# Loads, norm sums, reloads and reads moved around the dense stages of a two-block layer kernel

## The chip, the cores and the metric

The kernel runs on one core of one Trainium2 chip. The metric is the device time of one execution in microseconds (us); lower is better. TensorE does the matmuls, VectorE, ScalarE and GpSimd the elementwise work, and SyncE (SP) issues most of the loads. Every engine runs its own list of instructions in order and waits on semaphores for the others.

## The reference, cut to what matters

The input is x (1024 tokens of 1024 features, float32), with weights for five layers in a row. In short:

```
h = rmsnorm(x) @ w_in                  # split into 9 parts
oa = gated linear recurrence (4 heads) ; ob = banded attention (8 heads)
x = x + (sigmoid(ga)*(oa@wa) + sigmoid(gb)*(ob@wb)) @ w_out      # merge, wout
x = x + (silu(h2@w_gate) * (h2@w_up)) @ w_down                   # gu, dn
x = x + sigmoid(h3@w_ple_gate) * (p@w_ple_proj)                  # pleg
u = rmsnorm(x) @ w_in_a ; y = lru(conv(u[:1280])) * silu(u[1280:])
x = x + y @ w_out_a                                              # xg, wo1, wo2
c_kv, k_rope = split(rmsnorm(x)@w_dkv) ; cq, gate = split(rmsnorm(x)@w_in_b)
x = x + (causal attention with low-rank q, k, v * silu(gate)) @ w_out_b
out = rmsnorm(x) * final_norm
```

An rmsnorm multiplies each token by 1/sqrt(mean of its squares + eps) and each feature by a gain.

## The kernel before

All activations are kept transposed, as [128 features, chunk, 1024 tokens], eight chunks for the 1024 features. Tokens are worked on in two halves h of 512. A product of float32 is made from a high and a low part: ScalarE rounds a chunk to `..H` (ACT.Copy, with the norm's gain as scale), VectorE makes `..L` = x*gain - H, GpSimd splits each weight unit of 128x1024 in the same way (`split`), and TensorE does three matmuls of 128x128 by 128x512 per chunk and half: wH by H, wH by L, wL by H. The factor 1/rms of a token is not multiplied into the input but into the result, when VectorE reads it from PSUM. So a stage can begin before its norm is known, but the first read of its results cannot: the squares are made by ScalarE, added up chunk by chunk by VectorE in `square_sum` (acc), summed over the partitions by TensorE with a matrix of ones (`norm`), and turned into rstd by ScalarE with Ln and Exp.

The order of the stages is the table STREAM: za0, za1, zv, gates0, zqk, gates1, gates2, merge, wout, gu0 to dn2, proj, pleg, xg, wo1, wo2, dkv, cq, cgate, the attention's units, wob. A stage has units; a unit is one weight tile and gives 128 features, 48 matmuls for eight chunks. Units alternate between two pairs of PSUM banks, 0 and 1 or 2 and 3, so a unit can only start when VectorE has read the unit but one before it (`s_free`). Weights alternate between two slots too: `load_unit(u)` on SP waits for the split of unit u-2, and the split for the matmuls of unit u-2.

Five places matter here.

- The start. SP loads weight unit 0, then x in four DMAs of two chunks (`s_x`). ScalarE first waits for `s_const`, which counts the constants vectors, identity and ones. TensorE does unit 0 of za0, then `norm(0, 0)`, then units 1 to 7.
- The gates. Results of gates2 are staged in `gates_staged_late` and stored to DRAM by `store_gates` on SP, in between the loads. The tile shares its bytes with chunk 3 of `o_band_low` (obL), so before VectorE writes that chunk it waits for the last stores (`s_gst`), and TensorE waits for the chunk (`s_ol`) ahead of the second part of the first merge unit. ScalarE, when gates2 is done, issues one DMA of 4 MB for x_mid.
- The end of the recurrent layer. `rnn_block(n)` on VectorE reads unit (n, 0) of xg, does the convolution of block n, `recurrence(n - 1)`, reads unit (n, 1) into rnn_gate, and makes `y_low(n - 1)`. Behind the loop come the reads of the first two units of wo1, `recurrence(9)`, `y_low(9)`, and the other reads. The residual x_late is loaded again by ScalarE's queue behind its loop.
- wo2 and dkv. `split_x(4, ...)` adds the results of wo2 to x_late and sums its squares; `split_x(5, ...)` then makes the parts of h_kv, `split_x(6, ...)` behind the norm those of h_mla, and VectorE reads dkv behind all of them.
- The last norm. `split_x(7, ...)`, `norm(5, 7)` and `norm_rstd(5)` follow the last unit of wob; then come eight products x_out of 1024 tokens, and four stores.

The regions R(0) to R(4) of 32 KB per partition hold one tensor of eight chunks each.

## Time and profile before

| | us |
|---|---|
| median of 3 runs (2760.71 to 2761.88) | 2760.83 |
| the profiled execution | 2760.46 |
| its span | 2758.5 |
| TensorE busy | 2638.1 |
| VectorE busy | 1273.2 |
| ScalarE busy | 768.5 |
| GpSimd busy | 879.1 |

The span is from the first to the last instruction or landing that was recorded; the execution's own time is 1.96 us longer. Busy times of engines overlap. Only what delays TensorE, or lies ahead of its first or behind its last matmul, shows in the time.

### The profile page before, as it was taken

The page shows a single profiled execution, that of the slowest core. Times are in us where ns is not written, and L with a number is a line of the kernel's source. Part 1 is how long each engine was busy: PE and PEld are TensorE (multiplying, and loading weights), DVE is VectorE, ACT ScalarE, POOL GpSimd, SP SyncE. Part 2 cuts the span into 40 slices and gives each one's busy share as a digit, 9 for nine tenths or more (in the row PEclk, how much of TensorE's full clock was granted, in tenths as well). Part 3 has the DMA queues.
Part 4 walks back from the last instruction along what each step waited for, and adds up shares of the span by engine and source line. Part 5 has one row for each costly group of instructions (what it writes and reads, how often), then busy time and mean ns, then how long its engine had stood idle before and what let it go on. Part 6 is the DMA issues. An engine that isn't in the chain of part 4 may idle for free.

```text
span 2758.5 us, 33222 instructions
## 1 busy us (share of the span) xinstructions
PE 2638.1 (96%) x13008; PEld 2179.0 (79%) x13008; DVE 1273.2 (46%) x1584; ACT 768.5 (28%) x1005; POOL 879.1 (32%) x660
## 2 busy tenths in 40 slices
PE   6999999899899999999999999999999899999996
PEld 5888887677688888888888877788877677888875
DVE  4474633466454322122212374668864323555543
ACT  5144244222221200000000122355531321444421
POOL 3453523211233333333333352333345223111111
PEclk9999999999999999999999999999999899999998
DMA  3101121111431111111111121211132211000021
GB/s 121 47 29 39 39 77 39 46 39 46 153 126 58 46 53 46 46 51 48 46 53 46 46 83 62 103 46 38 46 114 77 101 54 36 19 19 16 24 84 68
DMA packets 44498, 160.71 MB, mean 58 GB/s; under 512 B 4720, under 2 KB 9072, under 8 KB 41968
## 3 DMA queue, kind: packets, MB, share of 16 engines
q1 hardware_dynamic: 38336, 124.53, 13.4%
q10 hardware_dynamic: 6064, 34.78, 3.3%
q8 instruction: 72, 1.18, 0.2%
q14 instruction: 26, 0.21, 0.0%
HBM read 138.33 MB, written 20.97 MB: 58 GB/s over the span
## 4 chain that ended last, share of the span: by engine, by line
PE 84%; DVE 8%; ACT 4%; issue 3%; DMA 1%; ACTq 0%; DVEq 0%
PE ps L561 17%; PE ps L562 17%; PE ps L563 17%; PE ps L626 5%; PE ps L628 5%; PE ps L627 5%; PE ps L1004 2%; PE ps L691 1%; PE ps L786 1%; PE ps L806 1%; PE ps L994 1%; PE ps L794 1%; PE ps L922 1%; PE ps L924 1%; PE ps L923 1%
## 5 line engine op out<-in xcount | busy, mean ns | idle before, releaser
L441 POOL TENSOR_TENSOR derived_vectors<-w_staged 1x1 f32<-1x1 f32 x208 | 50.4, 242 | 1784.2 <-PE ps L563 1083.3
L444 POOL TENSOR_TENSOR w_low<-w_staged,w_high 128x1024 fp32r<-128x1024 f32 x208 | 557.3, 2679 | 16.7
L561 PE MATMUL ps<-h_ffn_high,w_high 128*128 128x512 f32 x832 | 324.6, 390 | 1.6 <-DVE ple_proj L1827 1.6
L563 PE MATMUL ps<-h_ffn_high,w_low 128*128 128x512 f32 x832 | 323.7, 389 | 0.0
L562 PE MATMUL ps<-h_ffn_low,w_high 128*128 128x512 f32 x832 | 323.7, 389 | 0.0
L626 PE MATMUL ps<-h_mix_high,w_high 128*128 128x512 f32 x688 | 282.1, 410 | 0.0
L628 PE MATMUL ps<-h_mix_high,w_low 128*128 128x512 f32 x688 | 269.1, 391 | 0.0
L627 PE MATMUL ps<-h_mix_low,w_high 128*128 128x512 f32 x688 | 268.4, 390 | 0.0
L442 POOL CAST w_high<-w_staged 128x1024 fp32r<-128x1024 f32 x208 | 215.0, 1034 | 0.0
L1809 DVE TENSOR_TENSOR squares<-ps,rstd 128x512 f32<-128x512 f32 x88 | 60.5, 688 | 322.1 <-PE ps L563 311.7
L561 PEld LDWEIGHTS ps<-h_ffn_high,w_high 128*128 128x128 f32 x832 | 156.2, 188 | 34.7 <-issue 2.5
L562 PEld LDWEIGHTS ps<-h_ffn_low,w_high 128*128 128x128 f32 x832 | 156.2, 188 | 32.8 <-issue 0.5
L563 PEld LDWEIGHTS ps<-h_ffn_high,w_low 128*128 128x128 f32 x832 | 156.2, 188 | 32.5
L628 PEld LDWEIGHTS ps<-h_mix_high,w_low 128*128 128x128 f32 x688 | 129.2, 188 | 28.1
L627 PEld LDWEIGHTS ps<-h_mix_low,w_high 128*128 128x128 f32 x688 | 129.7, 189 | 25.4 <-issue 1.5
L626 PEld LDWEIGHTS ps<-h_mix_high,w_high 128*128 128x128 f32 x688 | 129.8, 189 | 25.4 <-issue 1.5
L561 PE MATMUL ps<-act_high,w_high 128*128 128x512 f32 x352 | 136.9, 389 | 0.0
L562 PE MATMUL ps<-act_low,w_high 128*128 128x512 f32 x352 | 136.9, 389 | 0.0
L563 PE MATMUL ps<-act_high,w_low 128*128 128x512 f32 x352 | 136.9, 389 | 0.0
L561 PE MATMUL ps<-h_rnn_high,w_high 128*128 128x512 f32 x320 | 125.0, 391 | 1.6 <-DVE h_rnn_low L1452 1.6
L1479 DVE TENSOR_TENSOR x_mid<-ps,x_mid 128x512 f32 (+1 forms) x64 | 43.2, 686 | 178.2 <-PE ps L563 178.2
L563 PE MATMUL ps<-h_rnn_high,w_low 128*128 128x512 f32 x320 | 124.5, 389 | 0.0
(342 smaller groups left out, 5362.3 us busy)
## 6 DMA issues: line engine op xcount, KB each, us to landing
w_staged<-weights_in SPq DMA_DIRECT2D x200, 512.0 KB, 3.4
gates_loaded<-gates ACTq DMA_DIRECT2D x8, 1024.0 KB, 7.3
gates<-gates_staged_late SPq DMA_DIRECT2D x24, 256.0 KB, 2.0
x_in<-xT_in SPq DMA_DIRECT2D x4, 1024.0 KB, 9.4
x_mid<-xT_in ACTq DMA_DIRECT2D x1, 4096.0 KB, 12.9
x_spill_rnn<-x_mid ACTq DMA_DIRECT2D x8, 512.0 KB, 2.6
x_late<-x_spill_rnn ACTq DMA_DIRECT2D x4, 1024.0 KB, 7.8
x_spill_mla<-x_late ACTq DMA_DIRECT2D x1, 4096.0 KB, 11.1
```

What stands on the lines that cost most here:

```text
L441: nc.gpsimd.tensor_tensor(derived[0:1, 72:73], w_staged[0:1, j, 0:1], w_staged[0:1, j, 0:1], ALU.add)
L442: nc.gpsimd.tensor_copy(w_high[:, j], w_staged[:, j]).then_inc(s_wh, 1)
L444: nc.gpsimd.tensor_tensor(w_low[:, j], w_staged[:, j], f32(w_high[:, j]), ALU.subtract).then_inc(s_split, 1)
L561: nc.tensor.matmul(ps[:, bank], wH, rhs[0][:, r, tok], start=(n == 0), stop=False)
L562: nc.tensor.matmul(ps[:, bank], wH, rhs[1][:, r, tok], start=False, stop=False)
L563: last = nc.tensor.matmul(ps[:, bank], wL, rhs[0][:, r, tok], start=False, stop=last_chunk)
L626: nc.tensor.matmul(ps[:, bank], wH, h1H[:, c, tok], start=(c == 0), stop=False)
L627: nc.tensor.matmul(ps[:, bank], wH, h1L[:, c, tok], start=False, stop=False)
L628: done = nc.tensor.matmul(ps[:, bank], wL, h1H[:, c, tok], start=False, stop=(c == DC - 1))
L1004: last = nc.tensor.matmul(ps[:, 6, 0:P], v_mla[H // 2 % 2][:, k, (H % 2) * P:(H % 2 + 1) * P], mla.probsT[:, n % 2, k * P:(k + 1) * P], st ...
L1479: read(stage, i, j, h, lambda p: nc.vector.tensor_tensor(xm, p, xm, ALU.add))
L1809: read(stage, m, part, h, lambda p: nc.vector.tensor_tensor(sq[:, part, half_of(h)], p, rstd[:, half_of(h)], ALU.mult))
```

## The change

It has six parts.

1. Start: x comes in eight DMAs of one chunk with semaphores of their own, ScalarE and VectorE wait for vectors alone, the constant far_mask is dropped, and the first norm's sum stands behind the second unit of za0.
2. Gates: the stores of the last unit of gates2 are issued by ScalarE ahead of x_mid, no longer by SP.
3. Recurrent layer: the last block is taken out of the loops. In it VectorE reads the last unit of xg ahead of `recurrence(8)`, and ScalarE issues the reload of x_late behind the high part of the convolution.
4. wo2 and dkv: h_kv_high is made chunk by chunk behind the squares, and the low parts of chunks 0 to 3 behind the sums, within wo2. To have room, regions 1 and 4 change places for the tensors of the last layer, and the low parts lie four chunks further on (`low_chunk`). VectorE makes four low parts of h_mla, reads unit 0 of dkv, makes the other four, and reads on.
5. End: the last unit's square, sum, rstd, products and stores are done by halves of tokens; the sum of half 0 stands within the last unit (`between`).
6. Some semaphores have other names or are gone (s_invT, s_qnH).

```diff
 # SyncE
             for k in range(4):
-                sp.dma_start(x1[:, 2 * k:2 * k + 2], a["xT"][:, 2 * k:2 * k + 2]).then_inc(s_x[k], 16)
+                sp.dma_start(x1[:, 2 * k], a["xT"][:, 2 * k]).then_inc(s_xe[k], 16)
+                sp.dma_start(x1[:, 2 * k + 1], a["xT"][:, 2 * k + 1]).then_inc(s_x[k], 16)
...
-                    if 0 <= t < STAGE[stage][2]:
+                    if 0 <= t < min(STAGE[stage][2], 9):
                         store_gates(stage, t)
...
-            for h in range(4):
-                sp.wait_ge(s_fin, 2 * (h + 1))
-                sp.dma_start(a["outT"][:, 2 * h:2 * h + 2], out_sb[:, 2 * h:2 * h + 2]).then_inc(s_out, 16)
-            sp.wait_ge(s_out, 4 * 16)
+            for h in range(2):
+                for k in range(4):
+                    sp.wait_ge(s_fin, DC * h + 2 * (k + 1))
+                    sp.dma_start(a["outT"][:, 2 * k:2 * k + 2, half_of(h)], out_sb[:, 2 * k:2 * k + 2, half_of(h)]).then_inc(s_out, 16)
+            sp.wait_ge(s_out, 8 * 16)
 # TensorE
-            pe.wait_ge(s_const, 48)
             pe.wait_ge(s_split, 1)
             tile("za0", 0, 0, 0, P, 0, [(c, c) for c in range(DC)], (h1H, h1L), low(0))
+            unit_of("za0", 1)
+            pe.wait_ge(s_const, 32)
             norm(0, 0)()
-            for t in range(1, 8):
+            for t in range(2, 8):
                 unit_of("za0", t)
...
-            gemm("dkv", (h5H, h5L), low(5), norm(4, 4))
+            def kv_ready(r):
+                return (s_l, 32 + r + 1) if r < 4 else (s_l, 40 + r - 4 + 1)
+
+            gemm("dkv", (h5H, h5L), kv_ready, norm(4, 4), low_chunk=lambda r: (r + 4) % DC)
...
-            gemm("wob", (y7H, y7L), lambda r: (s_y7l, r + 1))
-            norm(5, 7)()
+
+            def last_sum(h):
+                pe.wait_ge(s_fsum, h + 1)
+                nc.tensor.matmul(ps[:, 4 + h], ones[:], acc[:, half_of(h)], start=True, stop=True).then_inc(s_nsum, 1)
+
+            gemm("wob", (y7H, y7L), lambda r: (s_y7l, r + 1), between_last=lambda: last_sum(0))
+            last_sum(1)
 # ScalarE
-            act.wait_ge(s_const, 48)
+            act.wait_ge(s_vec, 16)
             for m in range(DC):
-                act.wait_ge(s_x[m // 2], 16)
+                act.wait_ge((s_x if m % 2 else s_xe)[m // 2], 16)
...
+            for h in range(2):
+                act.wait_ge(s_free[bank_of("gates2", 9, h)], use_of("gates2", 0, 9) + 1)
+                act.dma_start(a["gates"][gate_unit("gates2", 9)][:, half_of(h)], gates_late[:, h]).then_inc(s_gst[h], 16)
             act.wait_ge(s_mm, MM_PER_UNIT * STAGE["merge"][0])
             act.dma_start(x2[:], a["xT"]).then_inc(s_x2, 16)
...
+            def x_reloaded():
+                act.wait_ge(s_mm, mm_count("xg", 2 * RB - 1, 1))
+                for k in range(4):
+                    act.dma_start(x4[:, 2 * k:2 * k + 2], a["x_spill_rnn"][:, 2 * k:2 * k + 2]).then_inc(s_x[k], 16)
...
                 nc.scalar.activation(convH[:], conv[:], ACT.Copy).then_inc(s_ch, 1)
+                if isinstance(n, int) and n == RB - 1:
+                    x_reloaded()
                 if not static:
                     y_high(n - 1)
...
-            split_x(4, x4, None, 0, updated("wo2"))
-            split_x(5, x4, h5H, G_KV, None, False)
+            split_x(4, x4, h5H, G_KV, updated("wo2"))
             norm_rstd(4)
-            split_x(6, x4, h6H, G_B, None, False)
+            split_x(5, x4, h6H, G_B, None, False)
...
-            split_x(7, x5, None, 0, updated("wob"))
-            norm_rstd(5)
+            split_x(6, x5, None, 0, updated("wob"), late=4, n=DC - 1)
+            act.wait_ge(s_l, 52 + 6)
+            for h in range(2):
+                act.wait_ge(s_free[bank_of("wob", 1, h)], use_of("wob", 3, 1) + 1)
+                nc.scalar.activation(sq[:, 1, half_of(h)], x5[:, DC - 1, half_of(h)], ACT.Square).then_inc(s_fsq, 1)
+                nc.scalar.activation(derived[0:1, 73:74], eps[0:1], ACT.Ln)
+                act.wait_ge(s_nsum, 2 * 5 + h + 1)
+                inverse_root([(rstd[:, half_of(h)], ps[:, 4 + h], 1.0 / D, s_rstd)])
 # VectorE
+                if last:
+                    project(n, 1, rgate)
                 if not first:
                     recurrence(n - 1)
-                project(n, 1, rgate)
+                if not last:
+                    project(n, 1, rgate)
...
-            split_x(4, x4, None, None, 0, add_to("wo2", x4))
-            split_x(5, x4, h5H, h5L, G_KV, squares=False)
+            def kv_low(m):
+                return nc.vector.scalar_tensor_tensor(out=h5L[:, (m + 4) % DC], in0=x4[:, m], scalar=V(G_KV + m), in1=f32(h5H[:, m]),
+                                                      op0=ALU.mult, op1=ALU.subtract)
+
+            for m in range(DC):
+                add_to("wo2", x4)(m // 2, m % 2)
+                dve.wait_ge(s_h, 32 + m + 1)
+                if m == 0:
+                    last = nc.vector.tensor_copy(acc[:], sq[:, 0])
+                else:
+                    dve.wait_ge(s_l, 32 + m)
+                    last = nc.vector.tensor_tensor(acc[:], acc[:], sq[:, m % 2], ALU.add)
+                if m < 4:
+                    last = kv_low(m)
+                last.then_inc(s_l, 1)
+            for m in range(4, DC):
+                kv_low(m).then_inc(s_l, 1)
...
+            query_low(0, 4)
             norm_rstd(4)
-            split_x(6, x4, h6H, h6L, G_B, squares=False)
...
+                    if k == 0 and t == 1:
+                        query_low(4, DC)
...
+            for h in range(2):
+                xm = x5[:, DC - 1, half_of(h)]
+                read("wob", 3, 1, h, lambda p: nc.vector.tensor_tensor(xm, p, xm, ALU.add))
+                dve.wait_ge(s_fsq, h + 1)
+                nc.vector.tensor_tensor(acc[:, half_of(h)], acc[:, half_of(h)], sq[:, 1, half_of(h)], ALU.add).then_inc(s_fsum, 1)
+            for h in range(2):
+                dve.wait_ge(s_rstd, 2 * 5 + h + 1)
+                for m in range(DC):
+                    nc.vector.scalar_tensor_tensor(out=out_sb[:, m, half_of(h)], ...)
```

TensorE's list around the first norm; rows 128x512 of h_mix are matmuls of za0, L609 and L611 the sum with ones. Before, behind the 48 matmuls of unit 0:

```order
L562 MATMUL ps<-h_mix_low,w_high 128x512
L563 MATMUL ps<-h_mix_high,w_low 128x512
L609 MATMUL ps<-square_sum,ones 128x512 x2
L626 MATMUL ps<-h_mix_high,w_high 128x512
L627 MATMUL ps<-h_mix_low,w_high 128x512
```

Afterwards the same sum stands behind 96:

```order
L629 MATMUL ps<-h_mix_low,w_high 128x512
L630 MATMUL ps<-h_mix_high,w_low 128x512
L611 MATMUL ps<-square_sum,ones 128x512 x2
L628 MATMUL ps<-h_mix_high,w_high 128x512
L629 MATMUL ps<-h_mix_low,w_high 128x512
L630 MATMUL ps<-h_mix_high,w_low 128x512
```

The sum has moved behind the 48 matmuls of unit 1.

VectorE's list at the end of the loop over the blocks of the recurrent layer, with the last lines of the loop's body. Before, the scan and the product of the recurrence come ahead of the two reads of rnn_gate:

```order
L1857 SCALAR_TENSOR_TENSOR rnn_r<-rnn_in,rnn_i 128x1024
L1859 REGISTER_ALU
L1861 REGISTER_ALU
L1861 TENSOR_TENSOR rnn_gate<-rnn_r,rnn_gate 128x1024
L1462 ISA
L1846 REGISTER_ALU
L1846 TENSOR_TENSOR rnn_gate<-ps,rstd 128x512
L1462 REGISTER_ALU
L1846 REGISTER_ALU
L1846 TENSOR_TENSOR rnn_gate<-ps,rstd 128x512
L1436 TENSOR_TENSOR rnn_y_low<-rnn_gate,rnn_y_high 128x1024
```

Afterwards, in the last block behind the loop, the two reads come ahead of the recurrence; the reads of wo1 into x_late are still behind it, and most of them behind the next one:

```order
L1458 TENSOR_TENSOR rnn_conv_low<-rnn_conv,rnn_conv_high 128x1024
L1868 TENSOR_TENSOR rnn_gate<-ps,rstd 128x512 x2
L1874 SCALAR_TENSOR_TENSOR rnn_r<-rnn_in,rnn_r 128x1024
L1877 TENSOR_TENSOR rnn_i<-rnn_i,rnn_r 128x1024
L1879 SCALAR_TENSOR_TENSOR rnn_r<-rnn_in,rnn_i 128x1024
L1883 TENSOR_TENSOR rnn_gate<-rnn_r,rnn_gate 128x1024
L1458 TENSOR_TENSOR rnn_y_low<-rnn_gate,rnn_y_high 128x1024
L1501 TENSOR_TENSOR x_late<-ps,x_late 128x512 x2
```

The reads of rnn_gate have moved from behind the recurrence to ahead of it; nothing else in the order of this place has.

VectorE's list between wo2 and cq. Before, eight low parts of h_mla (two, and a loop) stand ahead of the reads of dkv into squares (this tile holds the latent ckv there) and tmp:

```order
L1452 SCALAR_TENSOR_TENSOR h_mla_low<-x_late,vectors,h_mla_high 128x1024 x2
L143 UNCONDITIONAL_BRANCH
L143 ISA
L1452 ISA x2
L1452 SCALAR_TENSOR_TENSOR h_mla_low<-x_late,vectors,h_mla_high 128x1024
L1444 REGISTER_ALU
L1452 ISA x2
L1452 SCALAR_TENSOR_TENSOR h_mla_low<-x_late,vectors,h_mla_high 128x1024
L143 REGISTER_ALU
L143 COMPARE_AND_BRANCH
L1918 TENSOR_TENSOR squares<-ps,rstd 128x512 x4
```

Afterwards, behind the last sum, four low parts of h_kv, four of h_mla, the reads of unit 0, and the other four:

```order
L1948 TENSOR_TENSOR square_sum<-square_sum,squares 128x1024
L1938 SCALAR_TENSOR_TENSOR h_kv_low<-x_late,vectors,h_kv_high 128x1024 x4
L1957 SCALAR_TENSOR_TENSOR h_mla_low<-x_late,vectors,h_mla_high 128x1024 x4
L1968 TENSOR_TENSOR squares<-ps,rstd 128x512 x2
L1957 SCALAR_TENSOR_TENSOR h_mla_low<-x_late,vectors,h_mla_high 128x1024 x4
L1968 TENSOR_TENSOR squares<-ps,rstd 128x512 x2
L1968 TENSOR_TENSOR tmp<-ps,rstd 128x512 x2
```

The first reads of dkv have moved from behind eight low parts of h_mla to behind four, and four low parts of h_kv have left this place for wo2.

## Rows read from the trace of the kernel before

**Rows 1.** The page: busy time, share of the span and instructions.

```profile
PE 2638.1 (96%) x13008; PEld 2179.0 (79%) x13008; DVE 1273.2 (46%) x1584; ACT 768.5 (28%) x1005; POOL 879.1 (32%) x660
```

**Rows 2.** Waits of TensorE, longest first: total us, times, longest us.

```profile
PE ps L561 <- DVE h_mix_low L1452: 13.6, 1, 13.6
PE ps L609 <- DVE square_sum L1490: 10.6, 1, 10.6
PE ps L561 <- DVE o_band_low L1436: 9.0, 1, 9.0
PE ps L561 <- DVE squares L1918: 7.4, 1, 7.4
...
PE ps L561 <- DVE h_kv_low L1452: 6.1, 1, 6.1
PE ps L561 <- DVE rnn_gate L1846: 4.9, 1, 4.9
```

**Rows 3.** DMA issues: operation, count, KB each, median us to landing.

```profile
gates<-gates_staged_late SPq DMA_DIRECT2D x24, 256.0 KB, 2.0
...
outT<-x_out SPq DMA_DIRECT2D x4, 1024.0 KB, 4.1
...
vectors<-vectors_in ACTq DMA_DIRECT2D x1, 77.0 KB, 4.0
...
ones<-ones_in ACTq DMA_DIRECT2D x1, 64.0 KB, 9.2
```

**Rows 4.** The line that loads x_in.

```profile
DMA to landing us min/median/max: 6.1/9.4/12.5
```

**Rows 5.** Timeline of the start: start us, us, instruction, idle before it.

```profile
10.95 8.43 ACT L1074 ACTIVATE h_mix_high<-x_in,vectors 128x1024 fp32r<-128x1024 f32 x8 [2.33 <-DMA ones<-ones_in]
...
13.64 0.76 PE L561 MATMUL ps<-h_mix_high,w_high 128*128 128x512 f32 x1 [13.64 <-DVE h_mix_low L1452]
...
25.64 11.93 DVE L1490 TENSOR_TENSOR square_sum<-square_sum,squares 128x1024 f32<-128x1024 f32 x7
...
37.63 3.78 PE L609 MATMUL ps<-square_sum,ones 128*128 128x512 f32 x4 [10.62 <-DVE square_sum L1490]
...
45.22 1.29 DVE L1499 TENSOR_TENSOR z_hgrn_f<-ps,rstd 128x512 f32<-128x512 f32 x2 [7.64 <-ACT rstd L1053]
```

**Rows 6.** DMA issues from 740 to 760 us.

```profile
gates<-gates_staged_late SPq DMA_DIRECT2D x1, 256.0 KB, 12.3
```

**Rows 7.** Timeline of ScalarE's queue and VectorE, start of merge.

```profile
741.62 0.37 ACTq L1233 DMA_DIRECT2D x_mid<-xT_in  x1
...
754.75 1.23 DVE L1436 TENSOR_TENSOR o_band_low<-o_band,o_band_high 128x1024 fp32r<-128x1024 f32 x1 [12.37 <-DMA gates<-gates_staged_late]
```

**Rows 8.** Timeline of VectorE, end of xg and start of wo1.

```profile
2026.45 1.27 DVE L1846 TENSOR_TENSOR rnn_gate<-ps,rstd 128x512 f32 x2
...
2039.76 1.56 DVE L1852 SCALAR_TENSOR_TENSOR rnn_r<-rnn_in,rnn_r 128x1024 f32<-128x1024 f32 x1 [2.52 <-ACT rnn_r L1311]
...
2050.21 2.47 DVE L1479 TENSOR_TENSOR x_late<-ps,x_late 128x512 f32<-128x512 f32 x4
```

**Rows 9.** Timeline of VectorE, wo2 and dkv.

```profile
2114.68 2.58 DVE L1450 TENSOR_TENSOR square_sum<-square_sum,squares 128x1024 f32<-128x1024 f32 x1 [1.39 <-ACT squares L1039]
...
2137.53 9.64 DVE L1452 SCALAR_TENSOR_TENSOR h_kv_low<-x_late,vectors,h_kv_high 128x1024 fp32r<-128x1024 f32 x8
2159.36 12.64 DVE L1452 SCALAR_TENSOR_TENSOR h_mla_low<-x_late,vectors,h_mla_high 128x1024 fp32r<-128x1024 f32 x8 [12.18 <-ACT h_mla_high L1041]
```

**Rows 10.** Busy time by stretch; the number behind each engine's five is PEclk.

```profile
13.60:18.00 4.40, 4.36 (x10) 3.47 (x11) 4.40 (x4) 4.40 (x5) 1.29 (x2) 1.00 0.81 321
...
756.00:762.00 6.00, 5.97 (x14) 4.72 (x15) 1.62 (x3) 0.00 (x0) 0.00 (x0) 0.50 0.00 0
...
2100.00:2130.00 30.00, 30.00 (x134) 24.82 (x134) 17.35 (x13) 5.21 (x5) 16.74 (x14) 1.00 0.22 70
```

**Rows 11.** Timeline of VectorE, the last products.

```profile
2744.25 9.66 DVE L2025 SCALAR_TENSOR_TENSOR x_out<-x_last,vectors,rstd 128x1024 f32<-128x1024 f32 x8 [6.76 <-ACT rstd L1053]
```

More of the change, by code:

```diff
@@ L294, in fused_kernel @@
         s_free = [sem(f"bank{b}_read") for b in range(4)]
-        s_const = sem("constants_loaded")
+        s_const, s_vec = sem("constants_loaded"), sem("vectors_loaded")
+        s_xe = [sem(f"x_even_loaded{k}") for k in range(4)]
         s_x = [sem(f"x_loaded{k}") for k in range(4)]
@@ L547, in _, with tile @@
         def _(pe):
-            def tile(stage, i, j, slot, width, column, chunks, rhs, first_wait=None):
+            def tile(stage, i, j, slot, width, column, chunks, rhs, first_wait=None, between=None, low_chunk=None):
                 u0, t0, _, inc = base(stage)
@@ L561, in chunk @@
                     nc.tensor.matmul(ps[:, bank], wH, rhs[0][:, r, tok], start=(n == 0), stop=False)
-                    nc.tensor.matmul(ps[:, bank], wH, rhs[1][:, r, tok], start=False, stop=False)
+                    nc.tensor.matmul(ps[:, bank], wH, rhs[1][:, low_r, tok], start=False, stop=False)
                     last = nc.tensor.matmul(ps[:, bank], wL, rhs[0][:, r, tok], start=False, stop=last_chunk)
@@ L572, in tile @@
                         for h in range(2):
-                            chunk(h, n, c, r)
+                            chunk(h, n, c, r, low_chunk and low_chunk(r))
                 else:
@@ L577, in tile, with gemm, unit @@
                         for n, (c, r) in enumerate(chunks):
-                            chunk(h, n, c, r)
-            def gemm(stage, rhs, ready, hook=None, chunk0=0, after=None, after_limit=None):
+                            chunk(h, n, c, r, low_chunk and low_chunk(r))
+                            if between and h == 1 and n == 4:
+                                between()
+            def gemm(stage, rhs, ready, hook=None, chunk0=0, between_last=None, low_chunk=None):
                 u0, t0, n, T, C = STAGE[stage]
-                def unit(i, j, after=None):
+                def unit(i, j, between=None):
                     pe.wait_ge(s_split, 2 * i + (j + u0 + 1))
                     first = isinstance(i, int) and i == 0 and j == 0
-                    tile(stage, i, j, (u0 + j) % 2, P, 0, [(c, chunk0 + c) for c in range(C)], rhs, ready if first else None)
+                    tile(stage, i, j, (u0 + j) % 2, P, 0, [(c, chunk0 + c) for c in range(C)], rhs, ready if first else None, between, low_chunk)
                     if first and hook:
                         hook()
-                    if after and j == 1:
-                        after(i)
-                if after_limit is None:
-                    items_of(pe, n, lambda i, j: unit(i, j, after))
-                else:
-                    items_of(pe, after_limit, lambda i, j: unit(i, j, after))
-                    items_of(pe, n - 2, unit, after_limit)
-                    unit(n // 2 - 1, 0)
-                    return lambda: unit(n // 2 - 1, 1)
+                if between_last:
+                    items_of(pe, n - 2, unit)
+                    unit(n // 2 - 1, 0)
+                    unit(n // 2 - 1, 1, between_last)
+                else:
+                    items_of(pe, n, unit)
             def low(q):
@@ L1436, in low_of, with split_x @@
                 return nc.vector.tensor_tensor(L, source, f32(H), ALU.subtract)
-            def split_x(q, x, H, L, gain, before=None, after_h=True, squares=True):
+            def split_x(q, x, H, L, gain, before=None, squares=True, late=0, n=DC):
                 def chunk(i, j):
@@ L1871, in rnn_block @@
             def rnn_block(n):
-                first = isinstance(n, int)
+                first = isinstance(n, int) and n == 0
+                last = isinstance(n, int) and n == RB - 1
                 w = lambda k: vec[:, bass.ds(4 * n + (V_CW + k), 1)]
@@ L1895, in _ @@
             rnn_block(0)
-            with dve.Fori(1, RB) as n:
+            with dve.Fori(1, RB - 1) as n:
                 rnn_block(n)
+            rnn_block(RB - 1)
             for j in range(2):
```

94 lines of the change are left out of this document (47 added, 47 removed).

## The prediction

> **What bounds the kernel now.** I read the page first: TensorE is busy for 2638 of 2758 us [rows 1], so only its idle time, its time at the lower clock, and what lies behind its last matmul can be won. The waits of TensorE come next [rows 2]. Of its idle time the change can reach 13.6 us before the first matmul, 10.6 us before the first norm's sum, 9.0 us in the merge stage (wait for o_band_low), 6.1 and 7.4 us around dkv, and 4.9 us in wo1 (wait for the read of rnn_gate). Then the timeline of each place [rows 5 to 9], and last the granted clock. After a long wait the clock is at its lower level of the two, 1.2 and 2.4 GHz: 14 matmuls in 6.0 us, against 134 in 30 us in a stretch of unbroken work [rows 10]. So one matmul is 0.43 us there and 0.224 us (0.227 start to start) here, and a wait that ends in a low stretch of 6 us costs a further 14 x 0.205 = 2.9 us. A unit of eight chunks has 48 matmuls, 10.9 us; one of five chunks 30, 6.8 us.
>
> **Start (term A).** Before, ScalarE makes h_mix_high from 10.95, since it waits for all three constants; the slowest, ones, takes 9.2 us to land, vectors 4.0 [rows 3, 5]. Afterwards it waits for vectors and half of the first MB of x. The four pieces of 1 MB, issued one behind the other, land 6.1 to 12.5 us after issue [rows 4], the first at 7.3, the last at 15.4: 2.7 us a MB. I estimate the first half piece at 6.0, a table load of 1.3 behind it, and the first copy from 7.4. Matmuls then start near 9.9 instead of 13.64. They are slow for 4.4 us again (before, 10 matmuls in the first 4.4 us [rows 10]), then take 1.37 us a chunk: unit 0 ends at 22.9 and unit 1 at 33.8. The last piece of x lands at 15.4 as before, so the lows end at 17.9 and the sum chain starts there instead of at 24.9. Its seven additions took 11.93 us [rows 5]. A VectorE instruction of this shape alone is 1.2 us (eight in 9.64), and 2.58 when GpSimd splits a unit at the same time [rows 9]; seven with their squares are some 9.2 us, so 2.7 were lost to one split. Two splits now fall into the chain; I end it at 32, before unit 1 ends. The sum's matmuls run 33.8 to 35.6. From their end to the first read of unit 0 it was 45.22 - 41.41 = 3.8 us, and that read frees the bank of unit 2: TensorE idles from 35.6 to 40.1 instead of standing there for 10.6. Such a 4.9 us gap was followed by a low clock in wo1; I charge 2.3 us. Before, unit 2 started at 41.4 + 10.9 = 52.3; afterwards in effect at 42.4. **A = -10** (bounds: -6 when the chain overruns unit 1, -12.5 when the clock stays up).
>
> The Trainium skill (GPSIMD Engine Reference, Specifications) says that GpSimd and VectorE share SBUF interfaces and contend for VectorE instructions with two SBUF inputs; the additions of the sum and every low part are such. By it alone each of the seven could be held; holding all at 2.58 would end the chain at 36 and make A -8. The old row has one or two held of seven.
>
> **Merge (term B).** gates_staged_late shares its bytes with the last quarter of o_band_low. The last 256 KB store is issued by SP at 742.4, 0.8 us behind a 4 MB load of x_mid on ScalarE's queue (741.62), and lands after 12.3 us where the median store takes 2.0 [rows 3, 6, 7]; VectorE's low part starts at 754.75 and TensorE has waited 9.0. Afterwards both stores stand ahead of the load on ScalarE's own queue: landing at 744.5, VectorE held by GpSimd's split until 745.4, low part ready at 746.6, when part 0 of merge ends at 747.0. All 9.0 go, with the 2.9 of clock. The two sigmoids behind start 1.2 us later, which is hidden: the first is needed at 747. SP's loads are ahead of the old stores or wait for splits, nothing else is late. **B = -11.7** (bounds: 0 if the store still waits for the load, -12).
>
> **wo1 (term C).** VectorE reads unit (9,1) of xg ahead of the recurrence: possible at 2017.7 instead of 2026.45 [rows 8]. TensorE's second wo1 unit then starts at 2022.35, and the 4.9 us and some 2.3 us of clock are gone there. x_late is issued at about 2014.3, its 1 MB pieces land from 2019 on, not late. But look at what is late next. Unit 4 of wo1 needs a bank that VectorE only reads behind recurrence(9) and its y_low. That chain runs: rnn_gate of block 8, ScalarE's y_high, silu and decay (2026.5 to 2039.7), recurrence from 2039.76, and the reads at 2050.21. Nothing of it is moved forward; the two reads put ahead of recurrence(8) cost 1.28, of which GpSimd's split swallows half, so it ends 0.6 later. TensorE comes to the barrier 7.2 earlier and waits there from 2043.8 to 2051.5, 7.8 us, with a low clock behind it. Before it was there at 2050.1 at the high clock and waited 0.8. **C = +3.3**: 0.6 + 2.7 (bounds: +5, and -7.2 if the barrier moved too).
>
> **dkv (term D).** Before, the lows of h_kv start behind the last sum at 2137.53, dkv starts at 2138.9 after 6.1, and 5.5 us of low clock follow. Afterwards four of eight lows are made within wo2 (VectorE then has 1.4 of reads, 2.6 of sum and 1.2 of low in 6.8 us, so it keeps up) and h_kv_high lies in a region that nobody reads. TensorE starts dkv at 2132.85; lows 4 to 7 are ready at 2138.8, 2140.0, 2141.2 and 2142.4, so it waits about 0.5 and ends unit 0 at 2144.4 instead of 2152.5. The rstd is ready at 2149.9. VectorE makes four h_mla lows (1.27 each, paced by ScalarE) where before it made eight in 12.64 us [rows 9], reads unit 0 at 2156.1, and TensorE wants that bank at 2157.1: the 7.4 us and 2.9 of clock go too. The other four lows end near 2164.3 with one GpSimd split, and cq wants them at 2168. Unit 2 ends at 2168.0 instead of 2186.7. **D = -18.7** (bounds: -10 if one of the two gaps comes back, -19.5).
>
> **End (term E).** VectorE's x_out started at 2744.25 after 6.76 idle and ran 9.66 us, and the last of four 1 MB stores lands 4.1 us behind it [rows 3, 11]. Afterwards the sum of half 0 is a matmul pair inside the last unit (0.9 us more to wait for half 1: tile end 2735.0). Half 1 then has read, square and addition to 2737.1; x_out of half 0 can start there, since its rstd is ready at 2735.6. Sixteen products on 512 columns: no row shows one; between 0.60 (half of 1.21) and 0.69 (a read of 512 columns); I take 0.65: end at 2747.6 instead of 2753.9. ScalarE's second rstd is ready at 2740.7, before half 0 is out. The stores can begin behind two products at 2738.4 and move 4 MB; before, from the second product at 2746.7 to the end of the span at 2758.5 it was 11.8 us. That gives 2750.2; I add 0.8 for pieces of rows of 2 KB instead of 8. **E = -7.5** (bounds: -5, -8.5).
>
> The constant far_mask and its copy are 0.24 us on an idle ScalarE: nothing.
>
> **Sum.** -10 - 11.7 + 3.3 - 18.7 - 7.5 = -44.6. The profiled execution took 2760.46 around its span of 2758.5; the median is 2760.83, so 2716.2.
>
> **Rivals.**
> 1. The new wait in wo1 doesn't appear: the 7.2 us are kept. For it: [rows 2] name only the read of rnn_gate. Against: VectorE's 2.52 idle before 2039.76, released by ScalarE's root, shows the decay chain as the later bound. 2716.2 - 10.5 = 2706. Chance 0.08.
> 2. The gates' stores are still held by the 4 MB load, which now is issued 0.7 us behind them on the same queue. For it: 12.3 us for one of them. Against: that one was issued after the load, and 2.0 is the median of 24. B is 0: 2728. Chance 0.08.
> 3. VectorE, in order, is late once in dkv: reads of unit 0 stand 0.9 us before TensorE wants them, behind four lows and the norm. One gap of 7 to 9 us comes back: 2725. Chance 0.14.
> 4. Slower than before: behind one of the two gaps that I expect newly (36 to 40, 2044 to 2051) the clock does not come back within 6 us but stays at 1.2 GHz. In such a stretch work takes twice as long, so its price is half of its length; it decides at 89 us of it. Against: of the stretches at the low level none that I read is over 6 us of work [rows 10]. 2765 or more. Chance 0.02. The Trainium skill (TensorE: Matmul & The Clock Gate, Seeing it yourself) reports a clock stuck low for over 50 us; such a stretch here would give 25 us, 2741. No row shows one.
> 5. The forecast of five terms, each within its bounds: 0.68, own range 2710 to 2723.
>
> **Range and chances.** 2706 and 2728 are the rivals' times and hold 8 in 10 or a little more: 2707 to 2728. 5.5 us (0.2%) is about what can be told from no change. Cases 1, 2, 3 and 5 are all faster, less 0.02 kept for a stall that I don't see, half of it slower and half within the bound: faster 0.96; slower 0.03 with rival 4; same 0.01.
>
> **What would show it.** Right: first matmul near 10; a gap of 4 to 5 us before the third unit; no wait for o_band_low over 1 us; a wait of 7 to 8 us in wo1 for x_late; none over 1 us in dkv; x_out in 16 products ending some 6 us sooner after the last tile. Wrong: a store of gates over 5 us; TensorE waiting for h_kv_low, or for the reads of dkv; a low clock of over 10 us; x_out held by the stores.

## The result, and the profile after

The changed kernel takes 2714.78 us (median of 4 runs, 2714.23 to 2715.84), the kernel before beside it on the same chip 2760.77 (4 runs, 2759.73 to 2761.88): a ratio of 0.9834, 95% interval 0.9817 to 0.9851, so 46.0 us less. The forecast was 2716.2 with a range of 2707 to 2728. The span of the profiled execution went from 2758.5 to 2714.1 us, 44.4 less; the sum of the five terms was 44.6.

The page of the kernel after, its first line. It answers to [rows 1]: TensorE's busy time fell by 9 us only, and its share of the span rose from 96% to 97%. Most of what was won was idle time.

```profile
PE 2629.1 (97%) x13008; PEld 2173.5 (80%) x13008; DVE 1266.9 (47%) x1593; ACT 771.7 (28%) x1008; POOL 880.5 (32%) x660
```

Waits of TensorE after, longest first (total us, times, longest us). They answer to [rows 2].

```profile
PE ps L564 <- DVE h_mix_low L1474: 10.1, 1, 10.1
PE ps L564 <- DVE x_late L1501: 7.8, 2, 7.6
...
PE ps L628 <- DVE z_hgrn_f L1521: 4.6, 1, 4.6
...
PE ps L564 <- DVE h_kv_low L1938: 0.6, 1, 0.6
```

The wait for o_band_low (9.0) and that for the read of rnn_gate (4.9) are gone, and so is the one for the reads of dkv, `squares` (7.4). h_kv_low fell from 6.1 to 0.6, and the wait for the first norm's sum (10.6) became one for the read behind it, z_hgrn_f (4.6). New is x_late, 7.6 us in one piece: the "wait of 7 to 8 us in wo1" of the forecast.

DMA issues after (count, KB each, median us to landing), to set beside [rows 3].

```profile
outT<-x_out SPq DMA_DIRECT2D x8, 512.0 KB, 3.0
...
gates<-gates_staged_late ACTq DMA_DIRECT2D x2, 256.0 KB, 2.1
...
ones<-ones_in ACTq DMA_DIRECT2D x1, 64.0 KB, 6.8
```

Both stores of the last gates unit, now on ScalarE's queue ahead of the load of 4 MB, take 2.0 and 2.1 us. Before, the first of the two, issued on SP at 738.2, ahead of the load, took 2.0 us as well; only the last, issued 0.8 us behind the load, took 12.3 [rows 6]. The constant ones lands sooner as well, but nobody waits for it.

Timeline of the start after (start us, us, instruction, idle before it), to set beside [rows 5]; the rows are of ScalarE, VectorE, TensorE and GpSimd.

```profile
7.45 9.48 ACT L1084 ACTIVATE h_mix_high<-x_in,vectors 128x1024 fp32r<-128x1024 f32 x8
...
10.14 0.77 PE L564 MATMUL ps<-h_mix_high,w_high 128*128 128x512 f32 x1 [10.14 <-DVE h_mix_low L1474]
...
18.33 3.26 POOL L446 TENSOR_TENSOR w_low<-w_staged,w_high 128x1024 fp32r<-128x1024 f32 x1
...
19.26 2.89 DVE L1509 COPY square_sum<-squares 128x1024 f32<-128x1024 f32 x1
...
22.25 11.99 DVE L1512 TENSOR_TENSOR square_sum<-square_sum,squares 128x1024 f32<-128x1024 f32 x7
...
34.39 1.95 PE L611 MATMUL ps<-square_sum,ones 128*128 128x512 f32 x4
40.98 0.77 PE L628 MATMUL ps<-h_mix_high,w_high 128*128 128x512 f32 x1 [4.63 <-DVE z_hgrn_f L1521]
```

ScalarE begins at 7.45 (forecast 7.4) and TensorE at 10.14 (forecast 9.9). The first copy of squares starts at 19.26 under GpSimd's split and takes 2.89 us (0.68 in the trace of before); with the seven additions the chain ends at 34.24, not at 32, just before unit 1 ends. That was the luck of this execution: in seven of the eight other profiles whose sum stands behind unit 1, e9's of the same kernel among them, TensorE waits 0.5 to 1.0 us for the chain.

Timeline of VectorE after, end of xg and start of wo1, to set beside [rows 8].

```profile
1995.43 1.28 DVE L1868 TENSOR_TENSOR rnn_gate<-ps,rstd 128x512 f32<-128x512 f32 x2
...
2019.59 1.88 DVE L1874 SCALAR_TENSOR_TENSOR rnn_r<-rnn_in,rnn_r 128x1024 f32<-128x1024 f32 x1 [3.68 <-ACT rnn_r L1322]
...
2028.21 2.16 DVE L1458 TENSOR_TENSOR rnn_y_low<-rnn_gate,rnn_y_high 128x1024 fp32r<-128x1024 f32 x1 [1.12 <-ACT rnn_y_high L1308]
2030.30 2.47 DVE L1501 TENSOR_TENSOR x_late<-ps,x_late 128x512 f32<-128x512 f32 x4
```

The read of xg's last unit ends at 1996.7. The recurrence of block 9 still waits for ScalarE's root (3.68 us), and behind it and its low part stand the four reads, of which the first frees the bank that TensorE has wanted since 2023.5.

Timeline of VectorE after, end of wo2 and dkv, to set beside [rows 9].

```profile
2119.95 4.86 DVE L1938 SCALAR_TENSOR_TENSOR h_kv_low<-x_late,vectors,h_kv_high 128x1024 fp32r<-128x1024 f32 x4
2133.62 4.87 DVE L1957 SCALAR_TENSOR_TENSOR h_mla_low<-x_late,vectors,h_mla_high 128x1024 fp32r<-128x1024 f32 x4 [8.80 <-ACT h_mla_high L1052]
2138.41 1.28 DVE L1968 TENSOR_TENSOR squares<-ps,rstd 128x512 f32<-128x512 f32 x2
2139.61 7.91 DVE L1957 SCALAR_TENSOR_TENSOR h_mla_low<-x_late,vectors,h_mla_high 128x1024 fp32r<-128x1024 f32 x4
```

Four lows of h_kv are left behind the last sum. The lows of h_mla are cut in two by the read of dkv's unit 0; the second four take 7.91 us where the first take 4.87, since GpSimd splits a unit at the same time.

Timeline of the last products and their stores after, to set beside [rows 11].

```profile
2699.71 10.69 DVE L2082 SCALAR_TENSOR_TENSOR x_out<-x_last,vectors,rstd 128x512 f32<-128x512 f32 x16
...
2701.15 9.65 SPq L431 DMA_DIRECT2D outT<-x_out  x8
```

Positions of one and the same matmul in both traces show where the time went; each is the first matmul behind a wait of the kind that its row in the list of waits names. The last column gives the part of the shift that arose since the row above, by the terms A to E of the forecast. "Low stretch" stands for a stretch at the lower clock.

| place | before | after | shift | step |
|---|---|---|---|---|
| first of the scores in the band stage (wait 2.5) | 514.22 | 505.20 | -9.0 | A -9.0 |
| first wait of proj (3.6) | 1653.94 | 1634.09 | -19.9 | band +1.2, B -12.1 |
| first sum of dkv's latent (1.15) | 2200.42 | 2164.32 | -36.1 | C +2.2, D -18.5 |
| first matmul of wob (3.2) | 2644.25 | 2606.59 | -37.7 | -1.5 |
| end of the span | 2758.5 | 2714.1 | -44.4 | E -6.7 |

The band's +1.2 is the clock: behind the waits of 2.5 and 4.1 us there, which both kernels have, the low stretch ended some 3 us later after than before. The -1.5 is a low stretch at 2414 us that the trace of before has and the one of after has not. C and D are parted where wo2's last matmul ends, 2132.7 before and 2115.05 after.

### The profile page after: what moved, and what is told of

Read it like the earlier page. It is cut to its first block, busy times and chain, and to the rows that moved or that the text cites. A ratio compares the mean times of both kernels' runs of the same rounds, so it can differ in the third digit from the quotient of the medians.

```text
span 2714.1 us, 33080 instructions
## 1 busy us (share of the span) xinstructions
PE 2629.1 (97%) x13008; PEld 2173.5 (80%) x13008; DVE 1266.9 (47%) x1593; ACT 771.7 (28%) x1008; POOL 880.5 (32%) x660
## 4 chain that ended last, share of the span: by engine, by line
PE 86%; DVE 7%; ACT 3%; issue 2%; DMA 0%; ACTq 0%; DVEq 0%; SPq 0%
PE ps L564 18%; PE ps L565 18%; PE ps L566 18%; PE ps L628 5%; PE ps L630 5%; PE ps L629 5%; PE ps L1010 2%; PE ps L694 1%; PE ps L789 1%; PE ps L809 1%; PE ps L1000 1%; PE ps L797 1%; PE ps L928 1%; PE ps L930 1%; PE ps L929 1%
## 5 line engine op out<-in xcount | busy, mean ns | idle before, releaser
L565 PE MATMUL ps<-h_rnn_low,w_high 128*128 128x512 f32 x320 | 124.5, 389 | 0.0
```

Source lines behind the costliest of these rows:

```text
L565: nc.tensor.matmul(ps[:, bank], wH, rhs[1][:, low_r, tok], start=False, stop=False)
```

## The experiments

Ratios are to the kernel before on the same chip; its medians there were 2759.07 to 2761.01. Edits are against the changed kernel where nothing else is said. Single medians of the changed kernel differ by a few us (e9), so the smaller effects are read from positions in the profiles.

### e1 and e2: the recurrent layer's part alone, and all but it

e1 is the kernel before with part 3 of the change and nothing else; e2 is the changed kernel without part 3. The core of the edit (in e1 added, in e2 taken away):

```diff
 # VectorE
+                if last:
+                    project(n, 1, rgate)
                 if not first:
                     recurrence(n - 1)
-                project(n, 1, rgate)
+                if not last:
+                    project(n, 1, rgate)
 # ScalarE: the reload of x_late within the last block, behind convH
+                if isinstance(n, int) and n == RB - 1:
+                    x_reloaded()
```

> The kernel before with part 3 alone (the last block out of the loops, reads of xg's last unit ahead of recurrence(8), x_late reloaded earlier). Theory: the 4.9 us wait for rnn_gate goes, and a wait of 7 to 8 us for x_late comes before the fifth unit of wo1, with 2 to 3 us of low clock behind it, so the kernel is 1 to 4 us slower, 2762 to 2765. Rival (the wait is gone for good): 7 us faster, 2753 to 2754.

> The changed kernel with part 3 undone. Theory: the wait for rnn_gate of 4.9 us is back, that for x_late of 7.6 us gone, and the kernel is some 2.3 us faster than the changed one, 2711 to 2714. Rival (part 3 is worth its 7 us): 2721 to 2722.

e1 took 2758.99 us (2757.53 to 2760.83, 10 runs), ratio 0.9998 (0.9989 to 1.0008). e2 took 2716.84 (2715.10 to 2718.73, 4 runs), ratio 0.9844 (0.9828 to 0.9861). Neither theory's number came out: both lie between. The waits did move as forecast. One wait of TensorE in e1:

```profile
PE ps L561 <- DVE x_late L1485: 7.7, 2, 7.6
```

The wait for rnn_gate is gone and x_late took its place. From the wait of 1.6 us for h_rnn_low at the first unit of xg to the wait for h_kv_low in dkv it is 362.79 us in e1 against 360.75 before, and 362.90 in the changed kernel against 360.44 in e2. So the part costs 2.0 to 2.5 us where it stands, in both kernels. The medians hide it (e2's is even 2.1 us above the changed kernel's), since low stretches elsewhere differ between executions by as much: e2's profiled execution had one at 187 us, worth some 2.4 us, that the changed kernel's had not (last section). The theory (a cost) stands by sign and place, its size was too large by about 1 us, and the rival (a gain of 7) falls.

### e3: two reads ahead of the chain

If the new wait comes from the place of the reads behind recurrence(9), moving them ends it.

```diff
+            dve.wait_ge(s_x[1], 32)
+            add_to("wo1", x4)(1, 0)
             dve.wait_ge(s_ix, RB)
             recurrence(RB - 1)
+            add_to("wo1", x4)(1, 1)
             y_low(RB - 1)
-            for k in range(1, 4):
+            for k in range(2, 4):
```

> The changed kernel, and VectorE reads the third unit of wo1 ahead of recurrence(9) and the fourth between it and y_low(9). Theory (the reads wait only because they stand behind the recurrence in VectorE's order): the wait of 7.6 us and 2.4 us of low clock go, 2704 to 2706. Rival (the stage waits for the recurrence's result, not for the reads): the wait comes back one unit later, 2712 to 2715.

2707.05 us (2705.99 to 2707.68, 4 runs), ratio 0.9810 (0.9794 to 0.9826): 7.7 us below the changed kernel's median, and 1 us above the range of the theory. VectorE in e3, end of xg and start of wo1:

```profile
2016.75 1.88 DVE L1501 TENSOR_TENSOR x_late<-ps,x_late 128x512 f32<-128x512 f32 x3
2018.83 0.69 DVE L1501 TENSOR_TENSOR x_late<-ps,x_late 128x512 f32<-128x512 f32 x1 [0.20 <-PE ps L566]
2021.71 1.88 DVE L1874 SCALAR_TENSOR_TENSOR rnn_r<-rnn_in,rnn_r 128x1024 f32<-128x1024 f32 x1 [2.19 <-ACT rnn_r L1322]
...
2029.14 1.27 DVE L1501 TENSOR_TENSOR x_late<-ps,x_late 128x512 f32<-128x512 f32 x2
```

Of the reads ahead of the recurrence the last two are those of unit (1,0), in the gap in which VectorE waited for the decay; the two at 2029.14 are those of (1,1). TensorE's only wait in wo1 is one of 0.2 us, and the rival's wait one unit later does not come; between the same two places as in e1 it is 352.71 us, 10.2 less than in the changed kernel, as the theory had it (7.6 + 2.4). The chain of block 9 is no earlier: its recurrence starts at 2021.71 against 2019.59, and e3 entered this stage 2.15 us later, for the low stretch at 187 us that e2 has too; so its times show less than the 10.2 us. But nobody waits for the chain.

### e4: the last gates stores back on SP

```diff
-                    if 0 <= t < min(STAGE[stage][2], 9):
+                    if 0 <= t < STAGE[stage][2]:
 # ScalarE
-            for h in range(2):
-                act.wait_ge(s_free[bank_of("gates2", 9, h)], use_of("gates2", 0, 9) + 1)
-                act.dma_start(a["gates"][gate_unit("gates2", 9)][:, half_of(h)], gates_late[:, h]).then_inc(s_gst[h], 16)
```

> The changed kernel with the last two stores of gates2 back on SP's queue. Theory (the store is held because it reaches the DMA engines after the 4 MB load): it takes 12 us again, the wait for o_band_low of 9 us and 2.9 us of low clock are back, 2726 to 2728. Rival (the two queues share the engines fairly and the earlier time of the change decides): under 2720.

2728.39 us (2725.11 to 2731.16, 4 runs), ratio 0.9884 (0.9868 to 0.9901), 0.4 above the theory's range. SP's and ScalarE's queues, and VectorE, in e4 at the start of merge:

```profile
729.74 4.54 SPq L412 DMA_DIRECT2D gates<-gates_staged_late  x2
...
733.17 0.37 ACTq L1241 DMA_DIRECT2D x_mid<-xT_in  x1
...
733.25 0.69 DVE L1523 TENSOR_TENSOR gates_staged_late<-ps,rstd 128x512 f32<-128x512 f32 x1 [3.53 <-PE ps L630]
746.21 1.23 DVE L1455 TENSOR_TENSOR o_band_low<-o_band,o_band_high 128x1024 fp32r<-128x1024 f32 x1 [12.28 <-DMA gates<-gates_staged_late]
```

The low part waits 12.28 us for the store, as in [rows 7], and TensorE has its 8.9 us again. From the last wait of 0.6 us in the band stage to the first wait of proj it is 1038.2 us, against 1026.1 in the changed kernel and 1038.1 before: this edit undoes all 12.1 us of term B. It does two things at once, though. It puts the stores on SP, and ScalarE no longer waits for the last read before it issues the load. Both stores are on SP here: the first is issued at 729.74, 3.4 us ahead of the load, and lands after 2.0 us; the second is issued at 733.95, 0.8 us behind the load (733.17), and lands after 12.2. So SP's queue as such does not hold a store; the order against the load decides. Whether a store on SP issued just ahead of the load would be as fast as on ScalarE's queue was not tested.

### e5: the first norm's sum behind unit 0

```diff
-            unit_of("za0", 1)
             pe.wait_ge(s_const, 32)
             norm(0, 0)()
-            for t in range(2, 8):
+            for t in range(1, 8):
```

> The changed kernel with the sum of the first norm put back behind unit 0 of za0; the loads stay as changed. Theory (part of the start's gain comes from the place of the sum): TensorE ends unit 0 near 23.5 us and stands until the chain of additions ends near 34.3 us, a gap of 10 to 11 us; unit 1 then runs partly at the low clock (some 2.5 us more) and unit 2 starts near 49.5 us without a wait, where the changed kernel starts it at 41 us and loses 3.3 us to its own low clock. Cost about 5.3 us: 2719.5 to 2721. Rival (the earlier loads did all of it, the place of the sum is indifferent): 2714 to 2716.

2721.49 us (2718.59 to 2722.03, 4 runs), ratio 0.9864 (0.9847 to 0.9880). TensorE in e5:

```profile
34.38 3.74 PE L611 MATMUL ps<-square_sum,ones 128*128 128x512 f32 x4 [11.24 <-DVE square_sum L1511]
```

TensorE stands 11.24 us ahead of it (10.62 before the change), and the four matmuls of the sum take 3.74 us at the low clock. The same matmul of the band stage comes at 510.63 us, against 505.20 in the changed kernel and 514.22 before: 5.4 us of term A are the place of the sum (5.3 in the theory), 3.6 are the loads. The 3.3 us that the theory gave the changed kernel for its own low clock were 2.4: 12 matmuls from 40.98 to 46.08. The median is 0.5 above the theory's range. The rival falls.

### e6: the eight lows of h_mla in one piece

```diff
-            query_low(0, 4)
+            query_low(0, DC)
...
-                    if k == 0 and t == 1:
-                        query_low(4, DC)
```

> The changed kernel with all eight lows of h_mla on VectorE ahead of its reads of dkv, instead of four ahead and four behind the reads of unit 0. Theory (the split into four and four is needed, but only for part of the old gap of 7.4 us): the lows run from 2133.6 to about 2145, the first read ends near 2146 where TensorE wants that bank at 2143.4: a gap of 2 to 3 us and perhaps 1.7 us of low clock: 2717 to 2720. Rival (the order of these lows is what the whole gap of 7.4 us hung on): 2722 to 2725. Other rival (the reads are early enough anyway): 2714 to 2716.

2726.73 us (2726.34 to 2729.23, 4 runs), ratio 0.9884 (0.9868 to 0.9901). The first rival is right, though the time is 1.7 us above its range, and my theory is wrong. VectorE in e6:

```profile
2136.23 12.65 DVE L1957 SCALAR_TENSOR_TENSOR h_mla_low<-x_late,vectors,h_mla_high 128x1024 fp32r<-128x1024 f32 x8 [8.80 <-ACT h_mla_high L1052]
2148.80 2.47 DVE L1966 TENSOR_TENSOR squares<-ps,rstd 128x512 f32<-128x512 f32 x4
```

The eight take 12.65 us, not 11.4, since GpSimd splits a unit beside the last of them (from 2144.59 for 3.20 us). TensorE's wait behind them:

```profile
PE ps L564 <- DVE squares L1966: 7.3, 1, 7.3
```

7.3 us, nearly the 7.4 of before. My theory had also put TensorE's arrival at 2143.4, from the matmul at 2121.28 that follows the wait of 0.6 us; but dkv begins at 2115.05, the wait lies within its first unit, and TensorE arrives near 2139.7 in the changed kernel's time. There the read ends at 2139.69 (2138.41 + 1.28), so the order of the change is only just in time: the 0.9 us in hand that the prediction gave this read (2156.1 against 2157.1) were none. From the wait of 0.6 us to the first sum of the latent it is 52.8 us against 43.0: the order is worth 9.8 us, clock included.

### e7: all lows of h_kv behind the last sum

```diff
-                if m < 4:
-                    last = kv_low(m)
                 last.then_inc(s_l, 1)
-            for m in range(4, DC):
-                kv_low(m).then_inc(s_l, 1)
+            for m in range(DC):
+                kv_low(m).then_inc(s_kvl if m < 4 else s_l, 1)
...
-                return (s_l, 32 + r + 1) if r < 4 else (s_l, 40 + r - 4 + 1)
+                return (s_kvl, r + 1) if r < 4 else (s_l, 40 + r - 4 + 1)
```

> The changed kernel with all eight lows of h_kv behind the last addition of squares, instead of four of them inside wo2; h_kv_high stays where the change puts it. Theory: the first low ends at 2121.2, TensorE is there at 2115.0: a gap of 6.1 us in place of 0.6, and a low clock of some 6 us behind it (2.9 us): 2722 to 2724.5. Rival (the gap costs only itself, since the clock stays up): 2719.5 to 2721. Rival (highs ahead were enough, the lows are not the wait): 2714 to 2716.

2724.34 us (2721.52 to 2724.97, 4 runs), ratio 0.9870 (0.9854 to 0.9887). The wait of TensorE in e7:

```profile
PE ps L565 <- DVE h_kv_low L1939: 6.1, 1, 6.1
```

The 6.1 us are back. From the wait in wo1 to the first sum of the latent it is 139.84 us against 133.29: 6.5 us, of which 5.5 are the wait and 1 the clock. The median is in the theory's range, but the profile gives the clock less than the theory's 2.9 us: more than half of the low stretch lay within the wait (granted clock 0.69 in the wait, 0.77 in the 6.6 us behind it). Both dkv edits are needed; 9.8 + 6.5 us are most of D's 18.5.

### e8: four stores of whole rows

```diff
-            for h in range(2):
-                for k in range(4):
-                    sp.wait_ge(s_fin, DC * h + 2 * (k + 1))
-                    sp.dma_start(a["outT"][:, 2 * k:2 * k + 2, half_of(h)], out_sb[:, 2 * k:2 * k + 2, half_of(h)]).then_inc(s_out, 16)
+            for k in range(4):
+                sp.wait_ge(s_fin, DC + 2 * (k + 1))
+                sp.dma_start(a["outT"][:, 2 * k:2 * k + 2], out_sb[:, 2 * k:2 * k + 2]).then_inc(s_out, 16)
```

> The changed kernel, whose output is stored in four pieces of whole rows (1 MB each) that wait for both halves of x_out, instead of eight pieces by halves. Everything on the compute engines stays. Theory (at the end the transfer of 4 MB is as long as the products, so it must begin with the first half): the first store can go at 2706.4 us and from there it takes 11.8 us as before: the end is 4 us later, 2718 to 2720. Rival (VectorE's sixteen products set the end, the last store lands 4 us behind them in any form): 2714.5 to 2716.

2719.33 us (2718.26 to 2720.25, 4 runs), ratio 0.9854 (0.9838 to 0.9871). The end of e8:

```profile
2699.50 10.69 DVE L2081 SCALAR_TENSOR_TENSOR x_out<-x_last,vectors,rstd 128x512 f32<-128x512 f32 x16
...
2706.24 4.31 SPq L430 DMA_DIRECT2D outT<-x_out  x4
```

The products are where they were, 10.69 us, and the first store goes 5.1 us later than in the changed kernel; the span ends at 2718.0 instead of 2714.1. From the first store's issue it is 11.8 us to the end, as I took it from before. So at the end the transfer counts as much as the products, and the rival (the last store lands 4 us behind the products in any form) falls: here it lands 7.8 us behind them.

### e9: the changed kernel again, and e10: e3 with one product moved

e10 adds to e3:

```diff
                 read("wob", 3, 1, h, lambda p: nc.vector.tensor_tensor(xm, p, xm, ALU.add))
+                if h == 1:
+                    x_out(0, 0)
                 dve.wait_ge(s_fsq, h + 1)
```

> The changed kernel once more, with no edit, beside a variant of e3 on the same chip. In the profiles so far the stretches at the low clock differ between kernels even where nothing differs up to that point in time: e6, e7 and e3 show one at 188 us that the changed kernel's profile does not have, with a first matmul that starts 0 to 0.8 us later. Theory (these stretches vary from execution to execution, by 1 to 3 us of time in all): the median is 2713.5 to 2717.5 and at least one stretch of its profile stands elsewhere or is of another length. Rival (they belong to the kernel, each edit moves them): the profile shows the same stretches as before (39, 507, 1633, 2026, 2606, 2702 us), and 2714.2 to 2715.8.

> The kernel of e3_reads_ahead, and in addition the first of the sixteen products of x_out is made in VectorE's idle 0.7 us between its read of the last half tile and the addition of the last square, instead of behind it. Theory (VectorE's products and the stores behind them set the end): everything behind starts 0.6 us earlier, 2706 to 2707.5, below what the times can tell and to be read from the profile: the last product ends 10.0 us behind the last square's addition instead of 10.7. Rival (the product delays the addition, so the second root, and the end comes from there): the last product ends as late as before or later, 2707 to 2708.5.

e9 took 2718.65 us (2714.72 to 2721.13, 4 runs), ratio 0.9852 (0.9836 to 0.9869): the same kernel, 3.9 us above its first median, and 1.2 above what the theory allowed. Its profiled execution, on the other hand, has a shorter span, 2712.9, and its low stretches differ from those of the first, as these two pairs of windows show. The kernel after, at 38 and at 2024 us (length, busy us of each engine, PEclk, DMA share, GB/s):

```profile
38.00:48.00 10.00, 7.02 (x21) 5.60 (x22) 2.48 (x4) 8.41 (x12) 0.23 (x1) 0.66 0.34 105
2024.00:2036.00 12.00, 4.97 (x12) 3.96 (x13) 7.61 (x7) 1.06 (x1) 5.21 (x3) 0.57 0.13 44
```

The same kernel in e9:

```profile
38.00:48.00 10.00, 7.01 (x24) 5.64 (x25) 2.48 (x4) 8.41 (x12) 0.00 (x0) 0.83 0.33 105
2024.00:2036.00 12.00, 5.70 (x16) 4.56 (x17) 6.88 (x7) 1.06 (x1) 4.48 (x3) 0.72 0.13 44
```

With one kernel, the granted clock of the same stretch was 0.66 in one execution and 0.83 in the next. The rival (the stretches belong to the kernel) falls; the theory's range for the time was too narrow.

e10 took 2705.73 us (2704.51 to 2707.37, 4 runs), ratio 0.9805 (0.9788 to 0.9821), the fastest of all, though not to be told from e3 by its time, and 0.3 below the theory's range. VectorE and SP's queue at the end of e10:

```profile
2687.68 0.74 DVE L2079 SCALAR_TENSOR_TENSOR x_out<-x_last,vectors,rstd 128x512 f32<-128x512 f32 x1
2688.47 0.69 DVE L2089 TENSOR_TENSOR square_sum<-square_sum,squares 128x512 f32<-128x512 f32 x1
2689.08 10.02 DVE L2079 SCALAR_TENSOR_TENSOR x_out<-x_last,vectors,rstd 128x512 f32<-128x512 f32 x15
...
2689.85 9.65 SPq L431 DMA_DIRECT2D outT<-x_out  x8
```

From the start of the last square's addition to the end of the span it is 14.2 us (2688.47 to 2702.7), against 14.9 in e3 (2690.87 to 2705.8), and the last product ends 9.9 us behind the addition, against 10.6. The gain of 0.7 us is the length of the gap that the product now fills; the rival falls.

## Why the prediction was right, step by step

- **A, forecast -10, measured -9.0.** The start of the first matmul and the wait of 4.6 us behind the sum (4 to 5 forecast) are right. The low clock behind that wait cost 2.4 us (2.3 forecast). The sum chain ended 2.2 us later than I put it: 1.4 since the lows ended at 19.3 instead of 17.9 (the last took 2.16 us beside GpSimd's work), 0.9 in the chain itself. The two splits fell into it as forecast, but the first held the copy, not an addition, for 2.2 us. The chain stayed just in front of unit 1's end, so in this execution this cost nothing; in e9 it came 0.5 us late. It had no room left, so the bound of -6 was nearer than I thought. The missing 1 us is what TensorE was late by: unit 0 ended at 23.5 (22.9 forecast), the third unit began at 40.98 (40.1 forecast).
- **B, -11.7 against -12.1.** Right in its steps: moved by the 7.8 us with which the stage was entered, the landing comes 0.1 us and the low part 0.1 us off the forecast, and TensorE reaches the chunk 0.4 us behind it. e4 takes all of it back.
- **C, +3.3 against +2.2, +2.5 and +2.0** (trace, e2, e1). The mechanism is right: behind the old wait stood a later one on the same path that nothing moved (e3). Of the term 0.6 + 2.7 the first part did not come. The four reads begin at 2030.30, 19.9 us before the old 2050.21 [rows 8], just the shift with which the stage was entered.
- **D, -18.7 against -18.5.** Right, but with no room left: the read of unit 0 that the forecast put 0.9 us ahead of TensorE ends as TensorE arrives (e6). The two edits are worth 9.8 and 6.5 when each is undone alone. Rival 3 priced a gap that comes back at 9 us; e6 gives 9.8.
- **E, -7.5 against -6.7.** Moved by the 37.7 us with which wob was entered, the products start 0.3 us and the first store 0.4 us later than forecast; and from the first store's issue to the end it was 12.95 us (2701.15 to 2714.1) where I had 12.6 (11.8 and 0.8). A product on 512 columns takes 0.67 us in the sequence of sixteen, not 0.65. That the transfer is a bound there is shown by e8.
- **Not forecast:** +1.2 and -1.5 us of clock in stages that the change does not touch. They cancelled. By e9 such differences arise with no edit at all, so the agreement of the sum within 0.2 us is partly luck; the single terms agree within about 1 us. All eight executions of the changed kernel lie within 2714.23 to 2721.13.

Rival 1 fell by the wait of 7.6 us, rival 2 by 2.1 us per store, rival 3 by the missing wait for `squares`. Rival 4's clock that stays low did not occur in any profile. The mark of 10 us that the prediction set for a wrong forecast was touched, though, in a stage that the change does not touch: in the band stage after, the clock was low from 506.7 to 516.9 us, of which TensorE idled some 4 us.

## What to carry to other kernels

- A wait that is removed uncovers the next one on the same path. Ask what the instruction waits for that stands behind the moved one in the same in-order list; in wo1 the gain came only when the next reads, too, stood ahead of the slow instructions (part 3 alone costs 2 us, e1; with e3's move the place is 10.2 us shorter). Whether one of e3's two moves would have been enough was not tested.
- A small store that someone waits for must be issued ahead of the large load: 2.0 to 2.1 us on either queue here, against 12.2 and 12.3 when it was issued 0.8 us behind the load. One queue for both keeps that order by itself.
- At an end with products and stores of the same length, the transfer must begin with the first half of the results (3.9 us here, e8).

## What the runs showed of the hardware that was not expected

The clock fell where TensorE had hardly waited. In e3, and likewise in e2, e6 and e7, the granted clock was at its lower level for most of 187 to 195 us; in the changed kernel, e4, e8, e9 and e10 it was not. The two rows are of e3, where TensorE had been busy for 36.3 of the 37 us ahead; its waits of 0.31 and 0.34 us just before 184.30 and 186.64, each followed by 16 small matmuls (128x64), stand in the other profiles too:

```profile
150.00:187.00 37.00, 36.34 (x223) 32.00 (x223) 33.54 (x33) 18.22 (x24) 21.24 (x12) 1.00 0.09 29
187.00:195.00 8.00, 8.00 (x30) 6.81 (x30) 5.47 (x6) 0.80 (x2) 0.00 (x0) 0.57 0.00 0
```

The same stretch in e9:

```profile
187.00:195.00 8.00, 8.00 (x48) 6.97 (x48) 6.21 (x7) 1.14 (x3) 0.50 (x2) 1.00 0.00 0
```

30 matmuls against 48 in 8 us of unbroken work, the small ones included. From the third unit's first matmul (40.98 us in the changed kernel) to the wait of 2.5 us in the band stage it is 466.6 us in e2, e3, e6 and e7, 464.2 in the changed kernel and 463.5 to 464.8 in e4, e8, e9 and e10: the stretch costs 2 to 3 us, as much as term C. What sets it off stays open; no run was made for it.

VectorE's copy of squares has a single input in SBUF and was still held by GpSimd's split: 19.26 to 22.15 us, with the split from 18.33 to 21.59, where the trace of before shows 0.68 us for it without a split. The prediction had counted only instructions with two inputs. The Trainium skill (SBUF — State Buffer, SBUF: two separate sides) says that whichever of the two engines starts first has the shared ports for its whole instruction, and counts VectorE's two-port performance modes among those that need them; this trace agrees for the copy, which ended 0.56 us behind the split; that it ran in such a mode no run here shows by itself.
